# The ninth tile's prompt rows as one set of 128 attention rows instead of two sets of 32-row slots

## The reference, cut to what matters

```python
def stick_breaking(q, k, v, q_pos, k_pos, sb_bias):
    z = jnp.einsum('bqhd,bkhd->bhqk', q, k).astype(jnp.float32) * (HEAD_DIM ** -0.5)
    z = z + sb_bias.astype(jnp.float32)[None, :, None, None]
    visible = k_pos[None, :] < q_pos[:, None]
    log_beta = jax.nn.log_sigmoid(z)
    log_keep = jnp.where(visible, jax.nn.log_sigmoid(-z), 0.0)
    later = lax.cumsum(log_keep, axis=3, reverse=True) - log_keep
    a = jnp.where(visible, jnp.exp(log_beta + later), 0.0)
    return jnp.einsum('bhqk,bkhd->bqhd', a.astype(v.dtype), v)
```

## Time and profile before

| | |
|---|---|
| median of 3 runs | 1091.05 us (1089.43 to 1091.59) |
| the profiled execution: span from first to last instruction | 1090.1 us |
| the profiled execution's own time | no other figure than its span is kept; the median of the runs is 0.95 us above that |
| PE | 1045.2 us busy (96%), weight loads 826.0 us (76%) |
| DVE | 544.4 us busy (50%) |
| ACT | 309.3 us busy (28%) |
| POOL | 174.6 us busy (16%) |
| HBM | 290 GB/s over the span |
| granted TensorE clock, mean | 0.988 of full speed |

### The profile page before, as it was taken

The page is one execution under the profiler, slowest core; times in us unless marked ns, Lnnn a source line. Parts: engine busy times, 40 slices in busy tenths (PEclk is TensorE's granted clock), DMA queues, the critical chain, the costliest instruction groups (busy, mean ns, idle before and its releaser), DMA issues.

```text
span 1090.1 us, 29226 instructions
## 1 busy us (share of the span) xinstructions
PE 1045.2 (96%) x12774; PEld 826.0 (76%) x12774; DVE 544.4 (50%) x1052; ACT 309.3 (28%) x592; POOL 174.6 (16%) x160
## 2 busy tenths in 40 slices
PE   8999999999999999999999999999999988898996
PEld 7999999966666549899876898756898556565665
DVE  5327654378875543444734544555455534343431
ACT  6323332266775552222411011101110111101011
POOL 1001200599200000100010111111111111111102
PEclk9999999999999999999989999999999999999999
DMA  7356785000116467767899999999999999999994
GB/s 244 109 166 211 217 272 155 1 13 2 40 31 211 146 232 251 245 220 277 312 351 393 379 383 385 386 383 375 386 379 382 379 390 388 392 390 389 390 389 111
DMA packets 85816, 293.19 MB, mean 269 GB/s; under 512 B 13425, under 2 KB 44849, under 8 KB 60069
## 3 DMA queue, kind: packets, MB, share of 16 engines
q1 hardware_dynamic: 78277, 273.30, 67.2%
q0 software_dynamic: 7280, 17.58, 6.8%
q10 hardware_dynamic: 128, 0.39, 0.1%
HBM read 272.98 MB, written 42.87 MB: 290 GB/s over the span
## 4 chain that ended last, share of the span: by engine, by line
PE 73%; DMA 18%; DVE 4%; SPq 2%; ACT 1%; issue 1%; POOL 0%; ACTq 0%; POOLq 0%
PE bank L2827 20%; DMA w_all<-in_w_up 18%; PE bank L2375 12%; PE bank L2612 8%; PE bank L2418 4%; PE bank L2844 4%; PE bank L2584 3%; PE bank L2547 3%; PE bank L2848 3%; PE bank L2456 3%; SPq L1042 2%; PE bank L2852 2%; DVE keep L1887 1%; PE bank L2693 1%; PE bank L2479 1%
## 5 line engine op out<-in xcount | busy, mean ns | idle before, releaser
L2827 PE MATMUL bank<-w_all,xeT 128*32 128x256 f32 x6144 | 345.6, 382 | 22.2 <-DMA w_all<-in_w_up 19.2
L2827 PEld LDWEIGHTS bank<-w_all,xeT 128*32 128x32 f32 x6144 | 254.4, 111 | 107.0 <-issue 27.9
L2202 DVE STREAM_TRANSPOSE xeT<-xg 32x256 f32<-32x256 f32 x360 | 156.5, 435 | 97.0 <-DMA xg<-n_scr,tab 91.8
L2844 PE MATMUL bank<-w_all,hT 128*32 128x256 f32 x744 | 165.6, 379 | 0.0
L2848 PE MATMUL bank<-w_all,hT 128*32 128x512 f32 x744 | 129.3, 592 | 0.0
L1887 DVE TENSOR_TENSOR_SCAN keep<-keep,unseen 128x1024 f32<-128x1024 f32 (+7 forms) x64 | 94.8, 1514 | 37.8 <-ACT keep L1439 37.7
L2375 PE MATMUL bank<-w_hi,xh 128*128 128x256 f32 x376 | 108.1, 287 | 0.0
L2375 PE MATMUL bank<-w_hi,xl 128*128 128x256 f32 x376 | 105.5, 281 | 0.0
L2375 PE MATMUL bank<-w_lo,xh 128*128 128x256 f32 x376 | 105.5, 280 | 0.0
L2844 PEld LDWEIGHTS bank<-w_all,hT 128*32 128x32 f32 x744 | 81.8, 110 | 30.3
L1681 ACT ACTIVATE sgl<-bank 128x384 f32<-128x384 f32 x32 | 15.7, 490 | 304.2 <-PE bank L2827 304.2
(11 more groups left out here) (307 smaller groups left out, 1505.9 us busy)
## 6 DMA issues: line engine op xcount, KB each, us to landing
w_all<-in_w_down SPq DMA_DIRECT2D x64, 1024.0 KB, 30.2
w_all<-in_w_gate SPq DMA_DIRECT2D x64, 1024.0 KB, 32.6
w_all<-in_w_up SPq DMA_DIRECT2D x64, 1024.0 KB, 8.9
k_scr<-in_cache_k SPq DMA_DIRECT2D x32, 256.0 KB, 3.3
v_scr<-in_cache_v SPq DMA_DIRECT2D x32, 256.0 KB, 3.5
pgk<-k_scr SPq DMA_DIRECT2D x32, 256.0 KB, 3.9
w_raw<-in_w_in SPq DMA_DIRECT2D x7, 1024.0 KB, 7.1
pgv<-v_scr SPq DMA_DIRECT2D x4, 1024.0 KB, 6.6
```

What stands on the lines that cost most here:

```text
L2202: last = dve.transpose(xeT[i][rows_of(s), :, rows_of(g)], lane[:, :, s, :])
L2827: lasts = [pe.matmul(pair_ps(i)[rows_of(q), g, :, :], xeT[i][:, k, rows_of(g)], pair_of(b, i, k, q), start=(k == 0 and g != 1), stop=(k == ...
L2844: return pe.matmul(y_right_ps(g), hT[:, ft, rows_of(g)], w[ft // 2][:, ft % 2, DA:D], start=first and g != 1, stop=ends, skip_group_check= ...
```

## The change

The tail becomes one set of 128 rows: row `32 p + 16 a + r` is query `r` of head `2 p + a`. Its queries are first copied into a zeroed tile `qz_tail` of 128 rows by 4 pairs by 32 columns, where the even head's queries stand in partitions 0 to 63 and columns 0 to 15 and the odd head's in partitions 64 to 127 and columns 16 to 31, so one product over 128 rows gives both heads of a pair. DVE does this in turn 1 (`spread_tail`: one fill, two copies).

- Scores: 12 products of 128 rows by 32 columns (4 with 16 keys, 8 with 512), into `z_ps(0)` and a 16-column piece.
- One sigmoid pair, one mask, one scan; `i != TAIL` leaves out the second set on ACT and DVE.
- Transposes: 9 in three banks.
- Value products: 9 chunks by 4 pairs, 36 in all, with 128 weight columns and 32 moving columns; half of each result (a head's values times the other head's weights) isn't read.
- `hi_o` and `lo_o` of the tail: two operations of 64 rows instead of one of 128.
- The mask is made by DVE before the attention instead of by POOL at the start of the run (a fill and four selections leave POOL), and the tail's bias by a few more small DVE operations.
- Semaphore counts follow (`scored`, `rows_before`, `s_qz` now counts to 2).

```diff
+    qz_tail, at = place("qz_tail", [P, HP, 2 * TAILP], F32, at)
...
-            chain.link(pool.memset(tail_mask[:, :], 0.0))
-            for j in range(4):
-                part = tail_mask[32 * j:32 * j + 32, :]
-                chain.link(pool.affine_select(out=part, in_=part, compare_op=ALU.is_gt, fill=1.0, base=0,
-                                              pattern=[[-1, TAILP]], channel_multiplier=1))
...
-                rows = slice(32 * (h % 4), 32 * (h % 4) + 32)
-                chain.done(dve.tensor_copy(bias_tail[rows, h // 4:h // 4 + 1], bias_bc[rows, h:h + 1]))
+                rows = slice(32 * (h // 2), 32 * (h // 2) + 32)
+                chain.done(dve.tensor_copy(bias_tail[rows, h % 2:h % 2 + 1], bias_bc[rows, h:h + 1]))
+            chain.done(dve.tensor_scalar(pint[:, 1:2], pint[:, 0:1], TAILP - 1, None, ALU.bitwise_and))
+            chain.done(dve.tensor_scalar(pint[:, 2:3], pint[:, 0:1], 4, 1, ALU.logical_shift_right, ALU.bitwise_and))
+            chain.settle()
+            chain.link(dve.tensor_copy(pflt[:, 6:8], pint[:, 1:3]))
+            chain.done(dve.tensor_scalar(tail_mask[:, :], col48[:, 0:TAILP], pflt[:, 6:7], None, ALU.is_ge))
+            chain.done(dve.tensor_scalar(pflt[:, 5:6], pflt[:, 7:8], -1.0, 1.0, ALU.mult, ALU.add))
+            chain.done(dve.tensor_tensor(bias_tail[:, 1:2], bias_tail[:, 1:2], pflt[:, 7:8], ALU.mult))
+            chain.settle()
+            chain.link(dve.scalar_tensor_tensor(out=bias_tail[:, 0:1], in0=bias_tail[:, 0:1], scalar=pflt[:, 5:6],
+                                                in1=bias_tail[:, 1:2], op0=ALU.mult, op1=ALU.add))
...
+            def spread_tail():
+
+                dve.wait_ge(s_ke, NQK)
+                dve.wait_ge(s_pr, ends[7])
+                chain.link(dve.memset(qz_tail[:, :, :], 0.0))
+                for a in range(2):
+                    rows = slice(64 * a, 64 * a + 64)
+                    last = dve.tensor_copy(qz_tail[rows, :, TAILP * a:TAILP * (a + 1)], qT[rows, :, row0(LAST):TP])
+                    if a == 0:
+                        chain.done(last)
+                last.then_inc(s_qz, 1)
...
-                if i < NU:
+                if i < NU and i != TAIL:
                     multiply(i, 1)
+                if i == 1:
+                    spread_tail()
...
-                    for a, lo, n in ((0, 1024, TAILP), (1, 1024, TAILP), (0, 0, 512), (0, 512, 512), (1, 0, 512), (1, 512, 512)):
-                        for j in range(4):
-                            h = 4 * a + j
-                            rows, cols = slice(64 * (h % 2), 64 * (h % 2) + 64), slice(32 * j, 32 * j + 32)
-                            z = z_tail_ps(a) if lo == 1024 else z_ps(a)[:, lo:lo + n]
-                            last = pe.matmul(z[cols, :], qT[rows, h // 2, row0(LAST):row0(LAST) + TAIL_Q],
-                                             kT[rows, h // 2, lo:lo + n], start=True, stop=True)
+                    pe.wait_ge(s_qz, 1)
+                    for lo, n in ((1024, TAILP), (0, 512), (512, 512)):
+                        for p in range(HP):
+                            rows = slice(2 * TAILP * p, 2 * TAILP * (p + 1))
+                            z = z_tail_ps() if lo == 1024 else z_ps(0)[:, lo:lo + n]
+                            last = pe.matmul(z[rows, :], qz_tail[:, p, :], kT[:, p, lo:lo + n], start=True, stop=True)
...
-                        pairs = [(h // 2, h % 2, h) for h in range(H)]
...
+                        for p in range(HP):
+                            last = pe.matmul(o_ps(t)[:, p, 0:2 * TAILP], values[:, P * p:P * (p + 1)],
+                                             x[:, 0, 2 * TAILP * p:2 * TAILP * (p + 1)], start=(c == 0 and p == 0),
+                                             stop=(c == ch[-1][0]), skip_group_check=True)
```

More of the change, by code:

```diff
@@ L372, in z_ps, with z_tail_ps @@
         return bank[:, 2 * a:2 * a + 2, :].rearrange("p b n -> p (b n)")
-    def z_tail_ps(a):
-        return bank[:, 6 + TAIL_TURN % 2, 8 * TAILP + TAILP * a:8 * TAILP + TAILP * (a + 1)]
+    def z_tail_ps():
+        return bank[:, 6 + TAIL_TURN % 2, 8 * TAILP:9 * TAILP]
     z_past_ps = bank[:, Z_PAST, :]
@@ L398, in last_unit, with heads, scored, rows_before @@
         return max(u for u in range(NU) if units[u][0] == t)
-    def scored(u):
-        return u + 1 if u < TAIL else u + 4
+    def heads(u):
+        return range(1 if u == TAIL else 2)
+    def scored(u, a):
+        return u + 1 if u < TAIL else u + (HP if a == 0 else 0)
+    def rows_before(u):
+        return 2 * u - (1 if u > TAIL else 0)
     def chunks(u):
@@ L419, in groups @@
             n = min(4, full - c)
-            found += [[(0, c, n), (1, c, n)]] if n <= 2 else [[(0, c, n)], [(1, c, n)]]
+            if u == TAIL:
+                found.append([(0, c, n)])
+            else:
+                found += [[(0, c, n), (1, c, n)]] if n <= 2 else [[(0, c, n)], [(1, c, n)]]
         if u == TAIL:
-            found.append([(0, LAST, 1), (1, LAST, 1)])
+            found.append([(0, LAST, 1)])
         return found
@@ L1422, in keep_head @@
                 w = width(u)
-                act.wait_ge((s_za, s_zb)[a], scored(u))
+                act.wait_ge((s_za, s_zb)[a], scored(u, a))
                 if u == 0:
@@ L1432, in keep_head @@
                 if u == TAIL:
-                    bias = bias_tail[:, a:a + 1]
+                    bias = bias_tail[:, 0:1]
                     act.activation(keep_of(u, a)[:, 0:2 * 512], z_ps(a), ACT.Sigmoid, bias=bias, scale=-HD ** -0.5)
-                    last = act.activation(keep_of(u, a)[:, 2 * 512:TP], z_tail_ps(a), ACT.Sigmoid, bias=bias,
+                    last = act.activation(keep_of(u, a)[:, 2 * 512:TP], z_tail_ps(), ACT.Sigmoid, bias=bias,
                                           scale=-HD ** -0.5)
@@ L1552, in hi_o @@
                 act.wait_ge(s_avb, last_unit(t) + 1)
-                r = P if t < LAST else TAILP
-                act.activation(cat_tile(HI, t)[:, HP:KT, 0:r], o_ps(t)[:, :, 0:r], ACT.Copy).then_inc(s_oh, 1)
+                if t < LAST:
+                    act.activation(cat_tile(HI, t)[:, HP:KT, :], o_ps(t), ACT.Copy).then_inc(s_oh, 1)
+                    return
+                for a in range(2):
+                    rows = slice(64 * a, 64 * a + 64)
+                    last = act.activation(cat_tile(HI, t)[rows, HP:KT, 0:TAILP],
+                                          o_ps(t)[rows, :, TAILP * a:TAILP * (a + 1)], ACT.Copy)
+                last.then_inc(s_oh, 1)
             def split_out_hi(n):
@@ L1577, in _ @@
                     copy_sums(0, range(0, 2))
-                if 0 < i < NU:
+                if 0 < i < NU and i != TAIL:
                     keep_head(i, 1)
@@ L1879, in multiply @@
                 back = row[:, ::-1]
-                dve.wait_ge(s_sg, 2 * u + a + 1)
+                dve.wait_ge(s_sg, rows_before(u) + a + 1)
                 if u == 0 and a == 0:
@@ L1923, in lo_o @@
             def lo_o(t):
-                r = P if t < LAST else TAILP
                 dve.wait_ge(s_oh, tiles.index(t) + 1)
-                dve.tensor_tensor(cat_tile(LO, t)[:, HP:KT, 0:r], o_ps(t)[:, :, 0:r],
-                                  cat_tile(HI, t)[:, HP:KT, 0:r].bitcast(F32), ALU.subtract).then_inc(s_ol, 1)
+                if t < LAST:
+                    dve.tensor_tensor(cat_tile(LO, t)[:, HP:KT, :], o_ps(t), cat_tile(HI, t)[:, HP:KT, :].bitcast(F32),
+                                      ALU.subtract).then_inc(s_ol, 1)
+                    return
+                for a in range(2):
+                    rows = slice(64 * a, 64 * a + 64)
+                    last = dve.tensor_tensor(cat_tile(LO, t)[rows, HP:KT, 0:TAILP], o_ps(t)[rows, :, TAILP * a:TAILP * (a + 1)],
+                                             cat_tile(HI, t)[rows, HP:KT, 0:TAILP].bitcast(F32), ALU.subtract)
+                    if a == 0:
+                        chain.done(last)
+                last.then_inc(s_ol, 1)
             def split_out_lo(n, k=slice(0, KT)):
@@ L2445, in scores @@
                 if u >= 1:
-                    pe.wait_ge(s_sg, 2 * u)
+                    pe.wait_ge(s_sg, rows_before(u))
                 if u == 0:
@@ L2461, in scores @@
                     pe.wait_ge(s_ur, 2)
[L2462 to L2468 removed]
+                    pe.wait_ge(s_qz, 1)
[4 more added lines that the diff above has]
+                            last = pe.matmul(z[rows, :], qz_tail[:, p, :], kT[:, p, lo:lo + n], start=True, stop=True)
                             if lo == 512:
[L2470 removed]
+                                last.then_inc(s_za, 1)
             def past_keys(k, samples):
@@ L2483, in new_scores @@
                 if g == 0:
-                    pe.wait_ge(s_qz, 1)
+                    pe.wait_ge(s_qz, 2)
                 else:
@@ L2541, in transpose_sums @@
                         free_bank(n)
-                        pe.wait_ge(s_p, 2 * u + 1 + group[-1][0])
```

(21 more changed lines are left out.)

3 lines of the change are left out of this document (1 added, 2 removed).

## The result

The changed kernel is slower: a median of 1097.67 us (8 runs, 1091.21 to 1099.85) against 1090.12 us (8 runs, 1087.78 to 1092.26) of the kernel before in the same session. The ratio is 1.0061, with a 95% interval of 1.0048 to 1.0074. The forecast was 1090.7 in a range that ended at 1093.6.

The account below looks back on a forecast made before the run. PE's queue in turns 3 to 6 of the attention was taken to decide. -1.7 - 2.75 + 3.25 + 0.8 = -0.4 us; 1090.1 - 0.4 + 0.95 = 1090.7 us, range 1088.5 to 1093.6.

Parts of the forecast that it names:

- Part 1: Tail's scores on PE in turn 4: 2.0 us instead of 3.7, so -1.7 us.
- Part 2: Transposes and wait for the tail's scan in turn 5: 5.1 us instead of 7.85, so -2.75 us.
- Part 3: Value products in turn 6: 72 records at 0.107 us, 7.7 us instead of 4.45, so +3.25 us.
- upper bound (+4.8): Highest cost allowed for turn 6's value products: +4.8 us, at 0.128 us a record.
- Part 4: Spread of the queries on DVE in turn 1, delaying PE's turn 3: +0.8 us, bounds 0 and 3.45.
- (1): Rival: turn 6's wide product isn't paced by its load, so Part 3 is 0; -3.65 us, 1087.4 us; chance 0.15.
- (2): Rival: POOL's long step gets between spread and unit 2's scan, Part 4 is 3.45 us; +2.25 us, 1093.3; chance 0.15.
- (3): Rival: turn 6 or 5 changes but a later wait takes it up; 1091.0 us; chance 0.07.
- (4): Rival: the new scores' four strips run one after the other; +5.5 us; chance 0.02.
- the last clause: Sign of a wrong forecast: turn 7 earlier or later by some us and the end not moved with it.
- What costs nothing: Small DVE steps before the attention (1.6 us) hidden in DVE's idle time; POOL, ACT and `hi_o`/`lo_o` changes also free.

Follow-up runs that it names:

- e2: The changed kernel with 64 moving columns instead of 32 in each of the tail's 36 value products: 1090.79 us, ratio 1.0005 to the kernel before.
- e1: The changed kernel with 128 moving columns instead of 32 in each of the tail's 36 value products: 1092.68 us, ratio 1.0018 to the kernel before.
- e8: The changed kernel with value products of chunks 0 to 4 as in the kernel before, only 5 to 8 wide: 1088.84 us, ratio 0.9985 to before.
- e6: The changed kernel with only the spread of the tail's queries moved ahead of DVE's first scan: 1095.53 us, ratio 1.0049 to the kernel before.
- e7: The changed kernel with value products of chunks 0 to 4 wide, 5 to 8 as in the kernel before: 1095.34 us, ratio 1.0041 to before.
- e5: The changed kernel with the old 72 narrow value products and the spread ahead of DVE's first scan: 1085.91 us, ratio 0.9957 to the kernel before.

## Why the prediction was wrong

**Part 1, right.** -1.7 foreseen, -1.78 measured; the scores took 1.99 us for the 2.0 foreseen.

**Part 2, right.** -2.75 foreseen, -2.86 measured: turn 5 takes 4.99 us for 5.1. The single tail scan ends at 251.37 + 2.33 = 253.70 and PE asks for it at 255.94, a slack of 2.2 us and not 0.6, mainly because the mask step took 0.69 us and not 2.0.

**Part 3 is the step that failed.** "72 x 0.107 = 7.7 us: +3.25 us" was right as far as it goes: at full clock the products run at 0.113 us a record, and turn 6 grows by 3.6 (e2). (The last 16 of the old records took 0.57 us, 269.00 to 269.57, and not 0.5.) It took every duration from rows at full clock and carried them over as if the clock were a constant of the kernel. With these products it fell. In the profiled execution that cost 17.16 - 11.65 = 5.5 us in turn 6 and 0.87 in turn 7, 6.4 in all. By the medians after is 7.55 us over its before and e2 0.14 over its own, so it is 7.4 us; against e1, which is 2.03 over its own, it is 5.5. Neither the upper bound (+4.8) nor any rival had a clock below 1.00 in it. Without the fall the sum would have come out near: I had said -0.4, the turns of e2, in effect the change at full clock, give +0.2, and its median +0.14 (e1's, +2.03, is further off).

**Part 4, inside its bounds.** +0.8 foreseen in turn 3, +1.28 measured. A POOL step held the copies, as the last section shows, so the three steps took 2.13 us (236.97 to 239.10) and not 0.6. The second scan of unit 2 ended at 241.39 + 3.06 = 244.45 us, inside the 243.9 to 245.5 named, though turn 3 began 0.76 us earlier than in before. In after and, last, in e8:

```profile
241.39 3.06 DVE L1921 TENSOR_TENSOR_SCAN keep<-keep,unseen 128x1024 f32<-128x1024 f32 x1
244.59 0.63 PE L2590 MATMUL bank<-ident,keep 128*128 128x128 f32 x4 [1.25 <-ACT qsum L1553]
```

```profile
241.39 2.27 DVE L1921 TENSOR_TENSOR_SCAN keep<-keep,unseen 128x1024 f32<-128x1024 f32 x1
```

The view puts PE's wait down to ACT's copy, which ended at 244.46; by the code these four transposes wait for that scan and for a bank that had been free since 240.68. The price hangs on POOL's order as well: in e8, with the same spread, POOL's long step began at 241.45 instead of 239.30, the scan took 2.27 us and turn 3 only 6.60, 0.43 more than before.

**The rivals.** (1), the wide product not paced by its load, is refuted by the 0.113 us a record, in e1, e2, e6 and e7. (2), POOL's long step in between, did not come at its price: that step (239.30, 4.81 us) ran beside the scans, and the second of unit 2 took 3.06 us where it took 2.38. (3) and (4) did not come either. The kernel is slower for a reason that none of them named. Of what I wrote would be the sign of an error, only the last clause came near: turn 7 later by 5 us, but with the end moved as well.

**What costs nothing.** Nothing in the traces speaks against this part (the small steps ahead of the attention are seven, not eight): but for the wait of turn 3 above, PE has no new wait on ACT, and e5 arrives at the 4.65 us that its turns say.

What makes the clock fall isn't settled. Shown, for turns 6 and 7: it fell in all three profiles that had 40 records in a row with 128 weight and 32 moving columns and in none of the seven that had not, two of them with the same loads and 64 or 128 moving columns; the length was another in each of the three (13.65, 3.41 and 10.24 us), one execution each. Only argued: that the one execution of after at 1091.21 us, with a mean clock of 0.990 where the seven others have 0.981 to 0.987, had a short fall or none. It wasn't profiled, and e6's execution of 1095.00 us with the same mean clock speaks against reading a time from it. A run that breaks up the 40 records with other work wasn't tried.

## What to carry to other kernels

Before a float32 product is widened to halve the count, compare what each form takes in weight loads: a pair of 64-column products passed in 0.124 us here (four records of 0.031) and the one 128-column product in its place takes 0.226 (two of 0.113), the same to 0.002 us with 64 or 128 moving columns. Read the granted clock in stretches of a few microseconds wherever products have few moving columns, in the kernel before as well: PE that shows busy throughout can still lose half its clock, and the bill comes in the work behind it. When a change has one bad part, take it apart: here the scores and the single scan without the wide value products, the spread put where DVE idles, give 0.9957 where the whole change gave 1.0061.

## What the runs showed of the hardware

The clock fell without any idle time. In after PE was busy 2.00 of 2.00 us in each stretch while the granted clock went from 1.00 to 0.50 and stayed there for 13.65 us, in e7 for 10.24, in e6 for 3.41. Late in after the clock falls behind a wait for a DMA:

```profile
904.17 2.26 PE L2869 MATMUL bank<-w_all,xeT 128*32 128x256 f32 x28 [2.58 <-DMA w_all<-in_w_up]
```

```profile
905.20:908.60 3.40, 3.40 (x39) 2.17 (x32) 3.27 (x9) 0.00 (x0) 0.38 (x1) 0.50 1.02 419
```

The Trainium skill, page TensorE: Matmul & The Clock Gate, section "HAM oscillation — how this bites in real kernels", explains falls by stretches in which TensorE waits for a DMA. The trace agrees at 905 us. Ahead of the falls of turn 6 in after, e6 and e7 there is no such wait; the traces show them with the engine full, so by that rule alone they would not have been foreseen.

Two copies of 64 by 64 floats took 1.93 us (from 237.17 on), where copies of that kind took under 0.2. A POOL step was running beside them, as POOL in order of time shows:

```profile
234.93 3.80 POOL L1191 TENSOR_TENSOR wsum<-wsum 128x1049 f32<-128x1049 f32 x1
238.69 0.35 POOL L1193 TENSOR_TENSOR wsmall<-wsmall 128x96 f32<-128x96 f32 x1
```

The long one ended at 238.73 and the short one at 239.04; DVE's first copy ended at 238.77 (237.17 and 1.60) and the second at 239.10. The Trainium skill, page SBUF — State Buffer, section "SBUF: two separate sides", says that the two engines' port pair is locked for a whole instruction; the trace now agrees for copies as well, which the earlier trace rows had shown for the mask step only.
